# A two-layer streaming encoder on one core: the order of work at the first projection, at the start and end of the attention, and at the output

## The reference, cut to what matters

```python
def run_trunk(x, ...):
    for layer in range(DEPTH):                     # 2 layers
        xn = rmsnorm(x, norm_mix[layer])
        if layer % 2 == 0:
            y, sa, sb = ab_mixer(xn, ab_w_in[li], ab_w_out[li], ...)
        else:
            y, rows = cd_mixer(xn, cd_w_in[li], fox_f_bias[li], cd_w_out[li], cache)
        x = x + y
        x = x + swiglu(rmsnorm(x, norm_ffn[layer]), ffn_w_in[layer], ffn_w_out[layer])
    return (rmsnorm(x, norm_final), ...)           # and states, keys, values

def dsa_attention(q, k_all, v_all, iq, iw, ik_all, q_start):
    score = jax.nn.relu(jnp.einsum('bqhd,bsd->bqhs', iqb, ik_all))
    score = jnp.einsum('bqhs,bqh->bqs', score, iwb) * IDX_SCALE
    _, idx = lax.top_k(score, topk)                # 128 keys of 512 for the prompt
    ...                                            # softmax over the chosen keys, times their values
```

## Time and profile before

| | before |
|---|---|
| time, median of 3 runs (lowest to highest) | 1448.52 us (1447.95 to 1449.59) |
| time of the profiled execution | 1446.89 us |
| its span, first to last instruction | 1445.2 us |
| busy: PE / DVE / ACT / POOL | 97% / 40% / 39% / 41% |
| mean granted TensorE clock | 0.991 |
| DMA, mean over the span | 79 GB/s |

### The profile page before, as it was taken

One profiled execution on the slowest core, in us unless ns is written; L12 is line 12 of the kernel. 1 busy time (PEld: TensorE's weight loads), 2 busy tenths in 40 slices (PEclk: granted clock), 3 DMA queues, 4 the chain that ended last, 5 costly groups with the idle time before them and its releaser, 6 DMA issues.

```text
span 1445.2 us, 27287 instructions
## 1 busy us (share of the span) xinstructions
PE 1400.5 (97%) x11034; PEld 1322.3 (91%) x11038; DVE 576.1 (40%) x1070; ACT 561.2 (39%) x909; POOL 588.0 (41%) x303
## 2 busy tenths in 40 slices
PE   8899999899999999999999989998999999999998
PEld 6688899799999999999989768777999999999997
DVE  6505556424431233123425966664643113311324
ACT  5635555434432243122355344443534223421222
POOL 4232222143545344534444456565244434453441
PEclk9999999999999999999999999999999999999999
DMA  5221122142233223322232322101133322332221
GB/s 178 74 69 51 50 77 63 37 128 88 88 87 103 73 87 88 102 73 73 74 110 71 88 75 74 44 27 44 36 108 87 106 71 87 87 104 73 80 66 62
DMA packets 204486, 114.34 MB, mean 79 GB/s; under 512 B 16500, under 2 KB 198648, under 8 KB 204408
## 3 DMA queue, kind: packets, MB, share of 16 engines
q1 hardware_dynamic: 199056, 109.47, 26.1%
q10 hardware_dynamic: 5352, 3.76, 0.8%
HBM read 107.26 MB, written 5.96 MB: 78 GB/s over the span
## 4 chain that ended last, share of the span: by engine, by line
PE 69%; issue 21%; POOL 7%; DVE 2%; ACT 1%; POOLq 0%; ACTq 0%; DVEq 0%
PE ps L1118 56%; POOL w_lo L584 6%; PE ps L1307 3%; PE ps L1253 3%; PE ps L1619 1%; PE ps L1268 1%; PE ps L1575 1%; PE ps L1587 1%; PE ps L1317 0%; PE ps L1730 0%; DVE small L2160 0%; PE ps L1611 0%; ACT arena L947 0%; POOL arena L566 0%; PE ps L1550 0%
## 5 line engine op out<-in xcount | busy, mean ns | idle before, releaser
L584 POOL TENSOR_TENSOR w_lo<-w_raw,w_hi 128x1024 fp32r<-128x1024 f32 x202 | 498.5, 2471 | 756.3 <-ACT w_hi L649 756.3
L1118 PE MATMUL ps<-x_hi,w_hi 128*128 128x272 f32 (+1 forms) x1840 | 384.6, 290 | 5.6 <-POOL w_lo L584 3.2
L1118 PE MATMUL ps<-x_hi,w_lo 128*128 128x272 f32 (+1 forms) x1840 | 381.6, 289 | 0.0
L1118 PE MATMUL ps<-x_lo,w_hi 128*128 128x272 f32 (+1 forms) x1840 | 380.3, 288 | 0.0
L1118 PEld LDWEIGHTS ps<-x_hi,w_hi 128*128 128x128 f32 (+1 forms) x1840 | 288.6, 188 | 12.6 <-issue 5.7
L1118 PEld LDWEIGHTS ps<-x_lo,w_hi 128*128 128x128 f32 (+1 forms) x1840 | 289.1, 188 | 0.5
L1118 PEld LDWEIGHTS ps<-x_hi,w_lo 128*128 128x128 f32 (+1 forms) x1840 | 287.1, 189 | 0.5
L649 ACT ACTIVATE w_hi<-w_raw 128x1024 fp32r<-128x1024 f32 x202 | 211.4, 1050 | 157.7 <-PE ps L1118 129.0
L1118 PE MATMUL ps<-o_hi,w_hi 128*128 128x272 f32 x832 | 173.1, 289 | 1.3 <-DVE arena L1994 1.1
L1118 PE MATMUL ps<-o_hi,w_lo 128*128 128x272 f32 x832 | 172.7, 289 | 0.0
L1118 PE MATMUL ps<-o_lo,w_hi 128*128 128x272 f32 x832 | 172.3, 289 | 0.0
(11 more groups left out here) (309 smaller groups left out, 1755.8 us busy)
## 6 DMA issues: line engine op xcount, KB each, us to landing
w_raw<-in_ffn_w_in SPq DMA_DIRECT2D x88, 512.0 KB, 3.7
w_raw<-in_ffn_w_out SPq DMA_DIRECT2D x32, 512.0 KB, 3.7
w_raw<-in_ab_w_in SPq DMA_DIRECT2D x28, 512.0 KB, 3.7
w_raw<-in_cd_w_in SPq DMA_DIRECT2D x13, 512.0 KB, 3.6
w_raw<-in_ffn_w_out SPq DMA_DIRECT2D x16, 384.0 KB, 3.4
w_raw<-in_ab_w_out SPq DMA_DIRECT2D x8, 512.0 KB, 4.2
arena<-in_x_prompt SPq DMA_DIRECT2D x4, 512.0 KB, 5.5
w_raw<-in_cd_w_in SPq DMA_DIRECT2D x8, 256.0 KB, 3.4
```

Source lines behind the costliest of these rows:

```text
L584: pool.tensor_tensor(wl[:, s, :], raw[:, s, :], wh[:, s, :].bitcast(F32), ALU.subtract).then_inc(lo_done, 1)
L1118: mm = pe.matmul(ps[0:M, b + h, 0:HALF], w[:, s, k * M:(k + 1) * M], xs[x][:, k, h * HALF:(h + 1) * HALF], start=(begin and k == ks[0] and ...
```

## The change

It keeps all arithmetic and moves work, in four places.

1. *First stage.* In `rms` the two small Ln come right behind the big one and the two Exp behind them, so that the table changes once and not three times. `hi(6)` moves ahead of the eight `x_hi` copies, `hi(7)` right behind them. The copy of `C_LR` moves ahead of `take_values(0, ...)`. PE computes the small job's tile of the first section's last part first, and ACT empties it first.
2. *Start of the attention.* POOL's `lo(DQ0)` and `lo(DK)` move behind the probabilities of x = 3. Two of the four search rounds of tile 1 that stood in between move ahead of the attention, and `chosen(1)` moves behind the two `sums`.
3. *End of the attention.* `last_rows(1, ...)` of step 25 moves ahead of its turns.
4. *Output.* PE turns the first three tiles of rows before `norm(4)`, the first seven feature tiles of two of them before the last one is scaled; the five tiles have banks `Y_BANK`; tiles 1 and 3 are scaled by ACT, 0, 2 and the small one by DVE. In the last `add_back` a square is added in its own turn, not one behind.

```diff
@@ gpsimd, attention
-                lo_after = {min(2 * s + 5, 2 * NX - 1): c for s, c in hi_at.items()}
+                lo_after = {min(2 * s + 5, 2 * NX - 1): [c] for s, c in hi_at.items()}
+                lo_after[3] = [C_DQ[0], C_DK]
...
-            for c in range(C_M1, C_DK + 1):
+            for c in range(C_M1, C_DQ[0]):
                 lo(c)
@@ scalar, first_norm
                 rms(0, 0)
+                hi(SLOTS + LEAD)
                 for k in range(KT):
                     act.wait_ge(s_nt, k + 1)
                     act.activation(xh[:, k, :], ntmp[:, k % NR, :], ACT.Copy).then_inc(s_nh, 1)
+                hi(SLOTS + LEAD + 1)
@@ scalar, behind first_norm
+            wait_done(act, C_LR)
+            jl = 2 * (jof[C_LR] % 2)
+            act.activation(two(lrT), ps[0:RANK, jl:jl + 2, 0:HALF], ACT.Copy).then_inc(frees(C_LR), 1)
             act.wait_ge(s_lb, 2)
             act.activation(cm[:, 4:12], cm[:, 4:12], ACT.Exp).then_inc(s_lb, 1)
...
             take_values(0, 0, rcol)
             pair_rows(0)
-            ahead(C_LR)
-            wait_done(act, C_LR)
-            jl = 2 * (jof[C_LR] % 2)
-            act.activation(two(lrT), ps[0:RANK, jl:jl + 2, 0:HALF], ACT.Copy).then_inc(frees(C_LR), 1)
@@ scalar, end
             rms(4)
+            act.wait_ge(s_rt, 5)
+            for i in (1, 3):
+                b = Y_BANK[i]
+                act.wait_ge(y_turned, i + 1)
+                act.activation(y_sb[:, i, :]..., ps[:, b:b + 2, :], ACT.Copy, scale=rcol[:, i:i + 1]).then_inc(y_scaled, 1)
@@ tensor, first_section
-                for i in range(NT + 1):
+                for i in [NT] + list(range(NT)):
@@ tensor, attention
+                    if s == 2 * NS - 1:
+                        pe.wait_ge(at_o, 9)
...
+                        last_rows(1, range(3), end=False)
                     if s < 2 * NS:
                         turn(2 * s)
                         turn(2 * s + 1)
@@ tensor, end
+            pe.wait_ge(x_scaled, KT - 1)
+            turn_x(0, range(KT - 1))
+            turn_x(1, range(KT - 1))
+            pe.wait_ge(x_scaled, KT)
+            turn_x(0, [KT - 1])
+            turn_x(1, [KT - 1])
+            turn_x(2, range(KT))
+            norm(4)
+            pe.wait_ge(s_rt, 3)
+            turn_x(3, range(KT))
+            pe.wait_ge(y_ready, 1)
+            turn_x(NT, range(KT))
@@ vector, attention
-                rounds([1], QUARTER // 2)
+                rounds([1], 1)
                 for x in range(2):
                     sums(x)
                 take_half(0)
                 for x in range(2, 4):
                     maxima(x)
-                rounds([1], QUARTER // 2)
-                chosen(1)
+                rounds([1], 1)
                 for x in range(2, 4):
                     sums(x)
+                chosen(1)
...
             chosen(0)
+            rounds([1], QUARTER // 2)
```

96 lines of the change are left out of this document (51 added, 45 removed).

## The result

| | before | after |
|---|---|---|
| time, median of 4 runs (lowest to highest) | 1448.72 us (1447.95 to 1449.59) | 1434.72 us (1433.35 to 1435.95) |
| time of the profiled execution, its span | 1446.89, 1445.2 us | 1434.03, 1432.3 us |
| mean granted TensorE clock | 0.991 | 0.994 |

The account below looks back on a forecast made before the run. PE was taken as the bound, busy 97% of the span, so gains come from its 45 us of standing and slower-clock stretches: 4.5 + 6.3 + 1.2 + 1.4 = 13.4, from 1448.52 to 1435.1 us, range 1431.5 to 1440.0.

Parts of the forecast that it names:

- Tables: First stage, ACT: two of four table loads of 1.28 go, so the norm's small steps end 2.56 us earlier.
- hi(6): First stage, ACT: moved in front it costs 1.05 us; the first x_hi still starts 1.3 earlier than at 42.27.
- (c): First stage: DVE's first x_lo waits for POOL's whole w_lo(6), so the x_lo chain is 0.3 us later, not 1.3 earlier.
- R3: Rival: DVE's x_lo and POOL's w_lo(6) overlap freely or POOL comes late; 0.9 us more gain, 1434.2; chance 0.12.
- (d): First stage, C_LR to gk: gk may start at 55.2; ACT reaches unit 0's first gate step 2.2 us earlier.
- (e): First stage, C_BV: PE ready at 68.1 waits until 70.0 for banks DVE frees; gain 4.5 us.
- R1: Rival: the lock race (L2011 behind w_lo(7)), the clock or chosen(1) takes back 1.2 to 3.5 us; chance 0.22.
- Start of the attention: Moving two w_lo on POOL removes PE gaps of 4.6 us and 1.7 of slow clock: 6.3 us.
- End of the attention: last_rows runs where PE stood 0.9 and 0.3: 1.2 us, bounds 0.9 to 1.4.
- Output: First output 0.55 us earlier, then DMA-bound at 403 GB/s for another 0.9: 1.4 us, bounds 1.1 and 1.7.
- R5: Rival: PE's time is given back later at a gap independent of PE; 1445.6 to 1448.5 us; chance 0.04.
- R4: Rival: slower, as a PE gap is followed by a much longer stretch at clock 0.50; chance 0.02.

Follow-up runs that it names:

- the last run: Fastest version (small rows ahead of C_LR's copy) with chosen(1) behind take_half(1) and POOL's two weight parts behind x = 1 instead of x = 3: 1436.34 us.
- e8_scan_free: Changed kernel with hi(6) behind the x_hi loop, the lower bounds' small operations ahead of the norm, and hi(8) behind unit 0's decays: 1434.42 us.
- a2_after_again: The changed kernel unaltered, profiled a second time: 1433.78 us.

## Why the prediction was right, point by point

- **Tables, hi(6), (c).** The first x_hi was forecast 1.3 ahead of 42.27 and came at 41.22; the first x_lo was to end at 44.0 and ended at 44.38; the last was to end at 52.8 and ended at 53.18. 0.3 of each is the later start of this execution. Taking w_lo(6) away restored 0.73, so the cause is shown. R3 is false.
- **(d).** gk at 55.68 for 55.2, its wait 1.54 for 1.5. Of the difference, too, 0.3 is that start (34.38 for 34.09).
- **(e).** C_BV 4.1 earlier on the clock, 4.38 counted from the norm's product (36.08 for 40.46), for 4.5. DVE's chain was the next bound as said, with 1.35 of idle PE ahead of it; 1.9 was forecast. The sum had PE ready 12.9 behind gk, and it was 13.4: the stretch of 6.8 us in before was put at 3.4, and such stretches cost 2.9 to 3.0 where the runs allow to tell. The error hid behind DVE's chain. The clock stayed up behind the 1.5 gap, as assumed, and did so in all five profiles of this code; but the reason given, a row elsewhere with a gap of 1.36, was no reason: two kernels with the same gap and two with 0.8 lost 1.3 to 2.9 us there. That the clock stayed up was therefore luck, though not much hung on it: a stretch of 3.4 us costs 1.3 there, and DVE's chain would have covered 1.35. R1's race was won by 0.08 us.
- **Start of the attention.** 6.53 for 6.3, 6.54 with that part alone. The two gaps are 4.59 of it; the stretch was put at 1.7, and others of its length cost 1.3 to 1.6, so that some 0.4 has no term. Both gaps and the 0.50 stretch went; POOL's queue of x = 4 and 5 hurt nobody. The moved rounds got no term, and VectorE's edits are worth 0.1. For chosen(1) the prediction let it end at the first boundary; in the changed kernel the case did not arise, and in the last run, where it did, it cost 1.0 and not 6.
- **End of the attention.** 1.41 for 1.2, at the upper bound of the range given (1.4). The term that was left out is the 0.24 of overlap between PE's rows, which the two waits had taken away.
- **Output.** 1.48 for 1.4, the first issue 0.6 earlier beyond the shift of what lies ahead (12.08 - 11.44; 0.55 forecast), DMA-bound to the end, shown with half of the bytes. The reason given for the other 0.9 was wrong: the hole in the old queue was put down to DVE's making the tiles one by one, and it was the clock of that profile, 0.8 us. Where no stretch lay there, the old code took the same 7.5 us from its first issue to the end. This term came out right by luck, since the profiled execution of before had that stretch and the changed one had not.
- **R5, "carried to the end unchanged".** All parts between are equal to 0.06 us, but for stretches at 0.50. R5 did not happen, and R4 neither. One reading for R5 was wrong: between 60 and 830 us a wait of PE of 1.57, at 346.51, ended with a weight part of POOL and not with a result of PE's own. It moved along with PE all the same (1.57 at 343.09 in the changed kernel).
- **The sum.** 13.4 forecast, 13.7 gained in the four parts, 12.9 by the spans, since 0.5 went to a longer stretch near 284 and 0.3 to a later start. The medians differ by 14.0: the offset of 1.6 between the median and the profiled run, which the prediction kept, was 0.7 in the changed kernel. That the forecast came within 0.4 us of the median is thus in part luck; two errors of 0.5 and 0.9 lay on opposite sides.

**What is open:** what decides whether a short gap of PE is followed by 0.50. The same code had other stretches in another execution. Those near 930 began 4.8 to 6.0 us behind PE's wait of 0.99, which every profile has. Those at 100 and 268 have no wait of PE over 0.15 us in the 30 us before them. The length of the gap alone is not it. Right before these two PE did products over few rows (64, 16 or 32 of 128), as here in e8_scan_free and in a2_after_again:

```profile
96.31 2.59 PE L1387 MATMUL ps<-arena 64*128 64x128 f32 x20
```
```profile
264.75 2.82 PE L1414 MATMUL ps<-arena 32*128 32x128 f32 x32
```

The same products stand there in the profiles without a stretch, and no run changed them, so that they have a part in it is not shown.

## What to carry to other kernels

Read the parts between fixed waits in both profiles, not only the spans: they repeat to 0.05 to 0.1 us and showed every edit here, while the median of the changed kernel moved by 1 us from one set of four runs to the next, and that of before lay between 1447.98 and 1451.28. Read the clock in both profiles before a gain is put down to an edit: 0.8 us of the output's 1.48 was a stretch that only the old profile had. Work that a second engine does for later (here weight parts on POOL) should be placed where neither its queue nor its SBUF port is wanted: moving two such pieces behind the first probabilities gave half of the whole gain. A cover that rests on the clock's staying up behind a gap is worth counting only as a chance, even where one profile shows it.

## What the runs showed of the hardware

- **A DVE operation caught by a POOL weight part waits for its whole rest.** x_lo went from 0.73 to 2.48, an operation on 4 columns from 0.17 to 1.73, the scan from 1.29 to 3.31, a tensor_scalar from 0.35 to 2.12. POOL waits for DVE as well: a weight part took 2.87 instead of 2.40, a multiply 1.34 instead of 1.24. The scan's 2 us stood in both kernels and was one of the two bounds of the first stage. The view of one source line shows such a case at once, by its greatest duration far above the median.
- **PE's clock falls to 0.50 while PE is fully busy, too,** at 100 to 104, 267 to 272 and 928 to 938 us, each for 3.4 to 6.8 us, in some executions and not in others of the same code. Those at 268 and 930 cost 1.4 to 1.5 us for 3.4 us, and 3.0 for 6.8. The spread of 2.6 and 3.7 us between four runs of the changed kernel is of the size of two of them.
- **The output leaves at 396 to 405 GB/s** with the DMA share at 1.02, and 24 transposes that took 4.5 us with 3.4 us of clock 0.50 over them took 3.5 at 1.00, waits included.
